# A third buffer for the weight sums of Strassen-like blocks, and its first copy one step earlier

## The reference

```python
z = rms(h) @ w_in;  h = h + concat(mixers(z)) @ w_out          # four small mixers
y = rms(h);         h = h + (silu(y @ w_gate) * (y @ w_up)) @ w_down
y = rms(h);         h = h + sigmoid(y @ w_ple_gate) * (p @ w_ple_proj)
x = rms(h)
x = x + attention_with_sinks(rms(x) @ swa_w_in) @ swa_w_out    # window of 128
```

## Time and profile before

| | us |
|---|---|
| median of 3 runs | 1379.96 (1379.74 to 1380.36) |
| the profiled execution | 1380.99 |
| its span, first to last instruction | 1379.2 |

### The profile page before, as it was taken

The page is one execution under the profiler, slowest core; times in us unless marked ns, Lnnn a source line. Parts: engine busy times, 40 slices in busy tenths (PEclk is TensorE's granted clock), DMA queues, the critical chain, the costliest instruction groups (busy, mean ns, idle before and its releaser), DMA issues.

```text
span 1379.2 us, 16905 instructions
## 1 busy us (share of the span) xinstructions
PE 1371.7 (99%) x6175; PEld 1123.2 (81%) x6175; DVE 1142.5 (83%) x1315; ACT 878.5 (64%) x1173; POOL 151.2 (11%) x127
## 2 busy tenths in 40 slices
PE   9999999999999999999999999999999999999998
PEld 7888888888888888788888888888888887777886
DVE  6589986688999988899999889976666769886897
ACT  7476755576777555677756576755566656675564
POOL 2000010011111000111100011100000144420000
PEclk9999999999999999999999999999999999999999
DMA  9766658887999788899987889999877878889675
GB/s 334 247 212 212 201 161 283 273 247 242 293 283 262 229 261 256 251 275 264 282 267 245 247 258 248 278 318 298 257 238 270 282 237 261 271 253 294 197 249 169
DMA packets 182859, 351.90 MB, mean 255 GB/s; under 512 B 13073, under 2 KB 37901, under 8 KB 182648
## 3 DMA queue, kind: packets, MB, share of 16 engines
q1 hardware_dynamic: 160408, 291.66, 64.4%
q0 software_dynamic: 9280, 33.97, 12.6%
q10 hardware_dynamic: 13088, 25.18, 6.1%
HBM read 296.19 MB, written 27.31 MB: 235 GB/s over the span
## 4 chain that ended last, share of the span: by engine, by line
PE 84%; DVE 2%; DMA 1%; issue 1%; ACT 0%; POOL 0%; ACTq 0%; DVEq 0%; POOLq 0%
PE acc L2340 13%; PE acc L2343 13%; PE acc L2342 13%; PE acc L2159 11%; PE acc L2161 11%; PE acc L2160 11%; PE sp L2340 2%; PE tp L2340 2%; PE tp L2343 2%; PE tp L2342 2%; PE sp L2343 2%; PE sp L2342 2%; DMA wide<-w_raw 1%; PE sp L2455 1%; PE tp L2471 1%; DVE w_lo L1391 1%
## 5 line engine op out<-in xcount | busy, mean ns | idle before, releaser
L963 ACT ACTIVATE w_hi<-w_raw 128x1024 fp32r<-128x1024 f32 x453 | 474.2, 1056 | 308.6 <-PE acc L2161 207.5
L1391 DVE TENSOR_TENSOR w_lo<-w_raw,w_hi 128x1024 fp32r<-128x1024 f32 x431 | 523.5, 1228 | 150.3 <-ACT w_hi L963 147.8
L2159 PE MATMUL acc<-w_lo,hh 128*128 128x512 f32 x528 | 207.7, 393 | 0.0
L2161 PE MATMUL acc<-w_hi,hl 128*128 128x512 f32 x528 | 205.6, 389 | 0.0
L2160 PE MATMUL acc<-w_hi,hh 128*128 128x512 f32 x528 | 205.6, 389 | 0.0
L2340 PE MATMUL acc<-w_lo,yh 128*128 128x512 f32 x452 | 176.0, 389 | 0.0
L2342 PE MATMUL acc<-w_hi,yh 128*128 128x512 f32 x452 | 175.9, 389 | 0.0
L2343 PE MATMUL acc<-w_hi,yl 128*128 128x512 f32 x452 | 175.8, 389 | 0.0
L963 ACT ACTIVATE w_hi<-wide 128x1024 fp32r<-128x1024 f32 x104 | 110.2, 1060 | 71.9 <-DVE wide L1405 35.7
L1391 DVE TENSOR_TENSOR w_lo<-wide,w_hi 128x1024 fp32r<-128x1024 f32 x104 | 126.8, 1223 | 13.7 <-ACT w_hi L963 13.4
L2159 PE MATMUL acc<-w_lo,yh 128*128 128x512 f32 x352 | 137.6, 391 | 0.3 <-DVE w_lo L1391 0.3
(11 more groups left out here) (332 smaller groups left out, 2179.4 us busy)
## 6 DMA issues: line engine op xcount, KB each, us to landing
w_raw<-in_w_gate SPq DMA_DIRECT2D x88, 512.0 KB, 5.8
w_raw<-in_w_up SPq DMA_DIRECT2D x88, 512.0 KB, 6.3
w_raw<-in_w_down SPq DMA_DIRECT2D x88, 512.0 KB, 6.3
w_raw<-in_w_in SPq DMA_DIRECT2D x64, 512.0 KB, 4.6
wide<-w_raw POOLq DMA_DIRECT2D x52, 512.0 KB, 6.0
w_raw<-in_swa_w_in ACTq DMA_DIRECT2D x48, 512.0 KB, 5.0
w_raw<-in_w_out SPq DMA_DIRECT2D x32, 512.0 KB, 5.9
w_raw<-in_w_ple_gate SPq DMA_DIRECT2D x32, 512.0 KB, 5.3
```

The lines of the kernel that those rows point to most:

```text
L963: act.activation(w_hi[:, v % SPL], src, ACT.Copy).then_inc(hi_ready, 1)
L1391: dve.tensor_tensor(w_lo[:, v % SPL], src, w_hi[:, v % SPL].bitcast(F32), ALU.subtract).then_inc(lo_ready, 1)
L2159: pe.matmul(dst, xh[:, f, tk], w_lo[:, v % SPL, k], start=(f == 0), stop=False)
L2161: last = pe.matmul(dst, xl[:, f, tk], w_hi[:, v % SPL, k], start=False, stop=(f == CK * end + CK - 1))
```

## The change

- There are two more buffers for weight sums, so that a set 3 needs neither of the two of `wide`: `big` (128 x 2048, idle in the gate/up pairs) for the pairs 1, 2, 4, 5, 6, 8, 9 and 10, and `both_tiles`, which lies over `tile6` and `tile7`, for the second block of the output projection. Sets 0, 1 and 2 use the halves of `wide` by their number. Pairs 3 and 7 and the down blocks are as they were.
- In these nine blocks ScalarE copies set 3's tops ahead of step 11, not of step 12. It waits for the buffer's last set, and additionally in pairs 4 and 8 for the down block before, and in the output block for `o_sums_low`.
- The semaphore of the adding DMAs is one for each buffer.

```diff
-              copied={0: [0], 3: [1], 9: [2], 12: [3]}, summed={0: 3, 1: 7, 2: 13, 3: 16})]
+              copied={0: [0], 3: [1], 9: [2], 11: [3]}, summed={0: 3, 1: 7, 2: 13, 3: 16}, spare={3: "tiles"})]
...
+for _m in range(1, PAIRS):
+    if _m % 4 != 3:
+        PAIR[_m].at = dict(PAIR[_m].at, copied={0: [0], 3: [1], 9: [2], 11: [3]}, spare={3: "big"})
...
+SUM_TILE = []
+for _block in BLOCKS:
+    if "summed" in _block.at:
+        SUM_TILE += [_block.at.get("spare", {}).get(_q, "wide%d" % (_q % 2)) for _q in _block.quads]
...
-        tile += [sb(f"tile{i}", [P, 1024]) for i in range(4, 8)]
+        tile += [sb(f"tile{i}", [P, 1024]) for i in range(4, 6)]
+        with ExitStack() as first:
+            both_tiles = first.enter_context(nc.sbuf_tensor("both_tiles", [P, D], F32))
+        tile += [sb(f"tile{i}", [P, 1024]) for i in range(6, 8)]
...
-            i = BY_DMA.index((a, b))
-            return wide[:, i % 2].rearrange("p (i n) -> p i n", i=4)
+            where = SUM_TILE[BY_DMA.index((a, b))]
+            whole = {"wide0": wide[:, 0], "wide1": wide[:, 1], "big": big[:], "tiles": both_tiles[:]}[where]
+            return whole.rearrange("p (i n) -> p i n", i=4)
...
-                pool.dma_start(wide[:, i % 2, CW:3 * CW], w_raw[:, u % RAW].rearrange("p k n -> p (k n)"),
-                               accum_op=ALU.add).then_inc(tops_added[i % 2], 16)
+                pool.dma_start(weight_sums(g, u)[:, 1:3].rearrange("p i n -> p (i n)"), w_raw[:, u % RAW].rearrange("p k n -> p (k n)"),
+                               accum_op=ALU.add).then_inc(tops_added[SUM_TILE[i]], 16)
...
-                if i >= 2:
-                    wait_low(act, SPLITS.index(("s",) + BY_DMA[i - 2]))
+                if SUM_TILE[i] in SUM_TILE[:i]:
+                    j = max(j for j in range(i) if SUM_TILE[j] == SUM_TILE[i])
+                    wait_low(act, SPLITS.index(("s",) + BY_DMA[j]))
+                if SUM_TILE[i] == "big":
+                    for r in range(2):
+                        if b is PAIR[4 * r + 4]:
+                            act.wait_ge(used, DOWNS[r][1].split("s", 1) + 1)
+                if SUM_TILE[i] == "tiles":
+                    act.wait_ge(o_sums_low, 1)
...
-                    dve.wait_ge(tops_added[i % 2], 16 * (i // 2 + 1))
+                    dve.wait_ge(tops_added[SUM_TILE[i]], tops_count(i))
```

More of the change, by code:

```diff
@@ L463, in build @@
         tops_copied = sem("tops_copied")
-        tops_added = [sem(f"tops_added{i}") for i in range(2)]
+        tops_added = {i: sem(f"tops_added_{i}") for i in ("wide0", "wide1", "big", "tiles")}
         m1_copied = sem("m1_copied")
@@ L599, in weight_sums, with tops_count @@
         def weight_sums(a, b):
-            i = BY_DMA.index((a, b))
-            return wide[:, i % 2].rearrange("p (i n) -> p i n", i=4)
+            where = SUM_TILE[BY_DMA.index((a, b))]
+            whole = {"wide0": wide[:, 0], "wide1": wide[:, 1], "big": big[:], "tiles": both_tiles[:]}[where]
+            return whole.rearrange("p (i n) -> p i n", i=4)
+        def tops_count(i):
+            return 16 * (SUM_TILE[:i].count(SUM_TILE[i]) + 1)
         def sums_of(v):
```

## The result

The changed kernel takes 1384.81 us (median of 6 runs, 1383.58 to 1385.51), the kernel before, on the same chip, 1380.07 (6 runs, 1379.65 to 1382.01): ratio 1.0029, 95% interval 1.0019 to 1.0040. It is slower by 4.7 us, between 2.6 and 5.5 by the interval. The profiled execution took 1385.51, its span 1383.8.

What follows compares the result with a forecast made beforehand. TensorE, busy 99% of the span, was taken as the bound, so only its gaps count. Six pairs lose 3.45 us and the earlier add gains 0: 1379.96 + 3.45 = 1383.4 us, range 1379.6 to 1384.9.

Steps and rivals of the forecast that it cites:

- The main term: PAIR[1], [2], [5], [6], [9], [10]: step 11's high part behind the copy delays VectorE 0.75 and TensorE's step 14; loses 3.45 us.
- 4 x 0.50: Pairs 1, 5, 9 and 10: step 14 starts 0.38 us late plus 0.12 of restart, 0.50 each, 2.00 together.
- 0.72: PAIR[2], with less slack: step 14 0.60 us late plus 0.12 of restart; PAIR[6] the same, 0.73.
- part of each falls at step 12; the sum is the same, as step 14 sets it: The six pairs with a transpose: step 12's slack goes first, but step 14 sets each pair's loss, 3.45 us together.
- the 0.12: TensorE behind a late operand: next matmul 0.11 us late, about 0.12 with the one after it.
- the transfers look served in the order in which they are ready: PAIR[4] and output block: set 3's add stays behind three loads, so issuing it 1.47 us earlier gains 0 (other end 2.49).
- Rival B: Add passes the third load, PAIR[4] and output block stalls vanish: 1380.9, chance 0.16; in one block only 1382.2, 0.10.
- C: Rival: VectorE's chain doesn't move or step 14 has more slack, no loss: 1377.5 without the stalls, 1380.0 with; chance 0.14.
- D: Rival: copy waits for a chunk, or delayed store and loads starve the next pair; 0.3 us more in five pairs: 1385, chance 0.07.
- "slower" at 0.48: Whole kernel: chance of slower by over 0.2%, 0.42 from the forecast case plus the rival of more harm; faster 0.03.
- 2.84 to 3.75: Bounds of the six pairs' loss in us, if ScalarE loses only 0.65 or 0.80 instead of 0.75.
- border of 2.76: Whole kernel: 0.2% in us, what a measurement can tell from no change; same reaches from 1377.2 to 1382.7.

## Why the prediction was right, and where it was not

*The main term: right in its mechanism, 0.4 us too small.* The copy at the old place of step 11, low 11 late by 0.75 (350.80, where the shifted time of before is 348.99 + 1.06 = 350.05), no idle until step 14, step 14 late by 0.39 for a forecast 0.38: each as written. The experiments confirm it from three sides: the move in the six pairs alone carries the loss, the buffer alone does not, and the transpose moved into VectorE's idle time takes it away. The size: 4 x 0.50 was 4 x 0.55, and 0.72 was 0.83 in PAIR[2] and PAIR[6] (mean of 0.84 and 0.82). The step that was short is "part of each falls at step 12; the sum is the same, as step 14 sets it". Step 14 does set the time, but TensorE then runs a few matmuls at 0.24 for 0.227 behind a restart, which the 0.12 did not hold in full; and in PAIR[2] the near miss of step 8 grew from 0.08 to about 0.15 (its operand is ready 0.05 ahead instead of 0.09). Measured 3.84 and 3.75 for 3.45.

*PAIR[4]: right.* The add issued earlier and landed no earlier: 10.33 us for a predicted 10.4, L1427's wait and the stall still there (1.28 and 1.47 for 1.31 and 0.92).

*PAIR[8] and the output block: wrong, and in opposite directions.* The prediction gave 0 to both. PAIR[8] lost 0.44 (0.40 by the second profiles), the output block gained 0.75 (0.40). The failed step is "the transfers look served in the order in which they are ready". It rested on the earlier trace rows, where one queue follows the other, and left out when the third load *landed*. In the kernel before, the third loads of PAIR[4] (issued at 555.03) and of PAIR[8] (at 802.88), and the add of PAIR[8] (KB, us to landing):

```profile
w_raw<-in_w_up SPq DMA_DIRECT2D x1, 512.0 KB, 9.6
...
w_raw<-in_w_up SPq DMA_DIRECT2D x1, 512.0 KB, 7.3
...
wide<-w_raw POOLq DMA_DIRECT2D x1, 512.0 KB, 7.6
```

In PAIR[4] the third load landed at 555.03 + 9.61 = 564.64, just 1 us ahead of the add that was "behind" it, though by 561.2 all but 0.05 of its 0.52 MB had been moved: this rest of it went along with the add's data (in 561.2 to 563.3, 30 packets of q1 beside 101 of q0). Of the three blocks only PAIR[8] had the two clean of each other, 810.14 and 812.52. In the changed kernel, PAIR[8], the same two and the queues from 813 to 816 us (packets, MB, share of 16 engines):

```profile
w_raw<-in_w_up SPq DMA_DIRECT2D x1, 512.0 KB, 10.4
...
big<-w_raw POOLq DMA_DIRECT2D x1, 512.0 KB, 9.6
...
q0 software_dynamic: 119, 0.45, 75.8%
q1 hardware_dynamic: 146, 0.29, 28.6%
```

Set out for all three blocks, from each DMA's issue and landing, in us from TensorE's start of step 14 (first profiles; "alone" is the version with the buffer alone, the copy at step 12):

| | third load issued, landed | add issued, landed |
|---|---|---|
| PAIR[8], before | -6.90, +0.36 | -4.82, +2.74 |
| PAIR[8], alone | -6.91, +3.08 | -5.35, +3.33 |
| PAIR[8], after | -6.92, +3.52 | -6.29, +3.26 |
| PAIR[4], before | -6.47, +3.14 | -4.81, +4.11 |
| PAIR[4], after | -6.47, +3.32 | -6.30, +4.03 |
| output block, before | -6.94, +4.25 | -4.82, +4.04 |
| output block, after | -6.90, +3.60 | -6.30, +3.26 |

Issued 2.08 behind the third load, PAIR[8]'s add went behind it; issued 1.56 or 0.63 behind, it shares the way with it, and both land late, the load by 3 us and the add by 0.5. (The output block's add of before was issued 2.12 behind its third load and shared all the same; there the two loads ahead of that one landed 1.7 us later than in PAIR[8]. So the distance alone doesn't decide.) In PAIR[4] the two shared already in the kernel before, and there an earlier issue changes nothing. The 0.5 us make PAIR[8]'s new stall, and the buffer alone brings it, in every profile with the third buffer and the loads not held (0.41 to 0.53). That it is the earlier issue and not the new place in memory is argued from the times at which the two queues move data; no run issues the add at its old time into the new buffer. Rival B held in no block in full: the add does not get the engines before the third load is served, it divides them with it. The version that holds the third load alone shows the other side: with no such partner the add of PAIR[4] lands after 6.66 us.

The Trainium skill (DMA: Bandwidth & Descriptors, section "Queues, rings and completion order") says that each engine goes round robin between the queues with work. The stretch from 813 to 816 agrees; that from 810 to 812, where q1 alone took the engines (101%), does not: the add had been issued at 807.24, and in the version with the held loads an add's first data moves 1.4 us after its issue. Whether the add's work stood ready in its queue behind the loads as early as that, no trace shows; if it did, this stretch differs from the page.

The output block's gain goes with the place of the copy, and so with the earlier issue: rival B was right there in part. TensorE's lost time in this block and the add's landing, counted as in the table, over all profiles in which the loads are not held:

| second output block | add issued | add landed | lost, us |
|---|---|---|---|
| before, two profiles | -4.82 | +4.04, +3.71 | 1.26, 0.96 |
| third buffer, copy at 12 (two versions) | -5.35 | +3.59, +3.73 | 0.85, 1.00 |
| half of the copy at 11 | -5.27 | +4.16 | 1.39 |
| third buffer, copy at 11 (four profiles) | -6.30 | +3.26 to +3.38 | 0.51 to 0.64 |

Issued 1.5 us earlier, the add lands 0.3 to 0.8 us earlier, where the forecast had nothing. Part of the rest is scatter in what is ahead in the queues: the first of the three loads landed at -0.90 where the add landed at +4.04, at -0.80 where it landed at +4.16, and at -1.26 to -1.67 in the others. Why the same earlier issue gains here and gains nothing in PAIR[4] is open.

*The sum.* By the first profiles +3.84 - 0.03 + 0.44 - 0.75 = 3.50 without the mixers, where 3.45 was forecast: in part luck, since a term too small by 0.4 met two unforeseen ones that nearly cancel. By the second profiles it is +3.75 + 0.55 + 0.40 - 0.40 = 4.30. The medians differ by 4.74, or by 4.85 from the 1379.96 on which the forecast of 1383.4 was built; it came out 1.4 below the measured time, which the range (to 1384.9) held by 0.1 only. About 0.4 of that is the main term, 0.1 the other median of the kernel before. The blocks account for 3.50 or 4.30 of the 4.74; what is left, 1.2 or 0.4 us, is not located, and lies inside the interval of the comparison.

*The rivals.* C (VectorE's chain stays) fell with the idle of 0.67. D expected more harm from a copy that waits for a chunk or from starving loads; the copy had no wait in any of the nine blocks, in either profile, and no gap of the six pairs stands elsewhere than at steps 8, 12 and 14. The chance of "slower" at 0.48 leaned on a loss of 2.84 to 3.75 against a border of 2.76; PAIR[8] was missing in it. The measured 4.7 lies beyond that border, to which "same" had been given 0.49.

## What to carry to other kernels

An instruction moved ahead on one engine moves another one back: price it on the engine behind, by following that engine's chain until its first idle time, and compare the chain's end with the moment at which the bottleneck engine wants it. If a transfer lands late while the DMA engines are full, look first at what stands ahead of it in the queues: four lines that hold back loads which nobody needs yet gave 2.2 us, and a buffer that lets the urgent transfer be issued earlier gave nothing in sum (0.4 to 0.75 won in one block, 0.4 lost in another). The place into which a delay puts idle time is also the place for work that can go anywhere, as the transpose here.

## What the runs showed of the hardware

- An adding DMA of 512 KB between two tiles of SBUF lands 5.5 to 5.6 us after its issue with no load ahead of it (4.8 to 4.9 in the versions that issue it 1.5 us earlier), 5.9 to 6.9 with two, 7.5 to 8.9 with three, and 9.5 to 10.6 if it is issued 1.5 us sooner behind the same three (each in PAIR[4], PAIR[8] and the second output block).
- Two transfers of different queues, issued 2.1 us apart, went one behind the other in PAIR[8], and landed 0.2 us apart in the output block; 1.7 us apart or less they divided the engines and landed within 1.3 us of each other, in PAIR[8] at the cost of 3 us for the first and 0.5 for the second.
- A matmul whose operand is late costs its waiting time and 0.11 us at the next start, with 0.01 at some of those behind; an operand that is ready 0.05 to 0.09 us ahead costs 0.08 to 0.16 as well (PAIR[1]'s step 12, PAIR[2]'s step 8, the half copy's step 14).
